# A trunk with a product-key expert layer: which gathered expert rows stand beside the choice of experts, and which engine takes them

## The reference, cut to what matters

```python
s = jnp.einsum('thpd,hpnd->thpn', q, sub_keys)
sv, si = lax.top_k(s, PEER_TOPK)
cand = (sv[:, :, 0, :, None] + sv[:, :, 1, None, :]).reshape(PEER_BLOCK, PEER_HEADS, PEER_TOPK * PEER_TOPK)
...
fs, fi = lax.top_k(cand, PEER_TOPK)
experts = jnp.take_along_axis(cidx, fi, axis=-1)
g = jax.nn.softmax(fs, axis=-1)
hid = jax.nn.gelu(jnp.einsum('td,thkd->thk', xb, u[experts]))
return jnp.einsum('thk,thkd->td', g * hid, v[experts])
```

## Time and profile before

| | us |
|---|---|
| median of three executions | 3921.12 |
| the profiled execution | 3898.55 |
| its span, first to last instruction | 3896.7 |
| VectorE busy | 2923.2 (75%) |
| TensorE busy | 2408.7 (62%) |
| GpSimd busy | 2397.6 (62%) |
| ScalarE busy | 531.2 (14%) |

### The profile page before, as it was taken

One profiled execution on the slowest core, in us unless ns is written; L12 is line 12 of the kernel. 1 busy time (PEld: TensorE's weight loads), 2 busy tenths in 40 slices (PEclk: granted clock), 3 DMA queues, 4 the chain that ended last, 5 costly groups with the idle time before them and its releaser, 6 DMA issues. The chain is left out here.

```text
span 3896.7 us, 29311 instructions
## 1 busy us (share of the span) xinstructions
PE 2408.7 (62%) x8928; PEld 1667.8 (43%) x8928; DVE 2923.2 (75%) x5647; ACT 531.2 (14%) x1237; POOL 2397.6 (62%) x2052
## 2 busy tenths in 40 slices
PE   8899527786798617767598717687788815600000
PEld 6676412464585313345486413355576513200000
DVE  2311786788877896778888797788777797798889
ACT  2310001122211101112110101122210101100000
POOL 0000377776675677766676577776566577777775
PEclk9989769997798859888698958998799968955555
DMA  4234699999899889999899989999799988999998
GB/s 176 96 107 140 213 324 361 369 392 348 294 408 409 339 316 347 368 384 392 325 389 409 352 321 347 361 390 391 291 365 409 370 323 308 355 350 367 368 387 339
DMA packets 359900, 1295.78 MB, mean 333 GB/s; under 512 B 40512, under 2 KB 40768, under 8 KB 359744
## 3 DMA queue, kind: packets, MB, share of 16 engines
q0 software_dynamic: 294912, 1073.87, 72.9%
q1 hardware_dynamic: 64256, 217.94, 14.8%
q10 hardware_dynamic: 576, 2.10, 0.1%
HBM read 1291.65 MB, written 2.10 MB: 332 GB/s over the span
## 5 line engine op out<-in xcount | busy, mean ns | idle before, releaser
L1057 POOL DMA_INDIRECT ring<-in_peer_u,eidx x1024 | 1222.6, 1194 | 960.1 <-DVE eidx L1181 475.1
L1057 POOL DMA_INDIRECT ring<-in_peer_v,eidx x1024 | 1174.8, 1147 | 516.8 <-issue 288.1
L1094 DVE CUSTOM_DVE_ANT_0 ring<-ring,hp 128x1024 f32<-128x1024 f32 x1024 | 1236.4, 1224 | 266.0 <-DMA ring<-in_peer_u,eidx 254.1
L1099 DVE SCALAR_TENSOR_TENSOR acc<-ring,wgt,acc 128x1024 f32<-128x1024 f32 x744 | 949.2, 1290 | 123.4 <-DMA ring<-in_peer_v,eidx 101.2
L519 PE MATMUL bank<-xt,panel 128*128 128x256 f32 x4096 | 952.8, 392 | 33.7 <-ACT raw L854 8.5
L519 PEld LDWEIGHTS bank<-xt,panel 128*128 128x128 f32 x4096 | 804.1, 198 | 164.0 <-issue 27.0
L752 PE MATMUL bank<-ring,dg 128*128 128x512 f32 x1120 | 549.6, 632 | 497.2 <-ACT dg L826 363.7
L752 PEld LDWEIGHTS bank<-ring,dg 128*128 128x128 f32 x1120 | 208.9, 198 | 825.4 <-issue 578.6
L594 PE MATMUL bank<-dg,ex 128*128 128x128 f32 x640 | 112.8, 349 | 149.2 <-DVE dg L1341 84.5
L594 PEld LDWEIGHTS bank<-dg,ex 128*128 128x128 f32 x640 | 105.4, 257 | 161.3 <-issue 145.7
L715 PE MATMUL bank<-yt,panel 128*128 128x256 f32 x768 | 173.6, 379 | 0.0
(11 more groups left out here) (164 smaller groups left out, 1884.0 us busy)
## 6 DMA issues: line engine op xcount, KB each, us to landing
panel<-in_panels SPq DMA_DIRECT2D x368, 512.0 KB
ring<-in_peer_u,eidx POOLq DMA_INDIRECT x1024
ring<-in_peer_v,eidx POOLq DMA_INDIRECT x1024
work<-in_rel_bias SPq DMA_DIRECT2D x16, 512.0 KB
gb<-in_ln_g SPq DMA_DIRECT2D x8, 512.0 KB
gb<-in_ln_b SPq DMA_DIRECT2D x8, 512.0 KB
panel<-in_keys SPq DMA_DIRECT2D x16, 256.0 KB
work<-in_x SPq DMA_DIRECT2D x4, 512.0 KB, 5.2
```

The lines of the kernel that those rows point to most:

```text
L1057: pool.indirect_dma_start(ring[:, n % RING, :], None, t_in["peer_u" if kind == "U" else "peer_v"], bass.IndirectOffsetOnAxis(ap=eidx[:, t, ...
L1094: v.tensor_tensor_reduce(row, row, hp[:, t, :], 1.0, 0.0, ALU.mult, ALU.add, hid[:, t, c:c + 1]).then_inc(used, 1)
L1099: stt(out=acc[:, t, :], in0=row, scalar=wgt[:, t, c:c + 1], in1=acc[:, t, :], op0=ALU.mult, op1=ALU.add).then_inc(used, 1)
```

## The change

Lanes 1 to 3 hold U rows of tile 0 of their own phase, 32 in each in phases 1 to 3, which VectorE dots with a copy of hp's tile 0 that ScalarE lays into PSUM (banks 4 and 5), and V rows of tile 1 of the phase before, which TensorE sums in banks 6 and 7. In phase 0 the lanes hold 40, 56 and 56 U rows, head by head and of both tiles; those of tile 0 use the PSUM copy. All other rows stand in the mixers, and what is left in the tail. The stream is written over phases: a V row may stand in the lanes after its own mixer. Sums are added once in a phase, for tile 1 alone, at the eighth row place of lane 3, followed by the layer norm of the phase before. Indices are kept for two phases. GELU and weights are made per head and tile.

```diff
+U_LANES = [(0, 40, 56, 56)] + [(0, 32, 32, 32)] * (PHASES - 1)
+V_LANES = [(0, 0, 0, 0), (0, 26, 26, 12)] + [(0, 40, 40, 16)] * (PHASES - 2)
+NORM_AT = 7
+def merged(a, b):
+    order = sorted([((2 * i + 1) * len(b), 0, i) for i in range(len(a))]
+                   + [((2 * i + 1) * len(a), 1, i) for i in range(len(b))])
+    return [(a, b)[j][i] for _, j, i in order]
...
+    rows, back = [], []
+    for p in range(PHASES):
+        n = sum(U_LANES[p])
+        if p:
+            u = of(p, "U", 0, range(HEADS)) + of(p, "U", 1, range(HEADS))
+        else:
+            u = [r for head in range(HEADS) for t in range(TILES) for r in of(p, "U", t, [head])]
+        lanes, u = u[:n], u[n:]
+        for it in range(1, LANES):
+            mine, lanes = lanes[:U_LANES[p][it]], lanes[U_LANES[p][it]:]
+            v, back = back[:V_LANES[p][it]], back[V_LANES[p][it]:]
+            beside = len(mine) // 2 if it == LANES - 1 and v else len(mine)
+            rows += merged(v, mine[:beside]) + mine[beside:]
+        v0, v1 = of(p, "V", 0, range(HEADS)), of(p, "V", 1, range(HEADS))
+        after = sum(V_LANES[p + 1]) if p + 1 < PHASES else 0
+        early = len(v1) - LAST // 2 - after if p + 1 < PHASES else 0
+        first = merged(v0[:len(v0) - LAST // 2], v1[:early])
+        rows += merged(first, u) + merged(v0[len(v0) - LAST // 2:], v1[early:early + LAST // 2])
+        back = v1[early + LAST // 2:]
+    rows += back
...
-LANE_ROWS = (0, 40, 64, 64)
-MIXER_ROWS = {"A": (16, 60), "B": (8, 32), "C": (12, 56), "G": (16, 64), "O": 16}
+LANE_ROWS = [[u + v for u, v in zip(U_LANES[s], V_LANES[s])] for s in range(PHASES)]
+MIXER_ROWS = [None, {"A": (12, 48), "B": (8, 28), "C": (8, 44), "G": (8, 60), "O": 16}] + [
+    {"A": (12, 52), "B": (8, 32), "C": (12, 48), "G": (12, 64), "O": 16}] * (PHASES - 2)
...
 def on_pe(n):
-    return kind == "V" and stage == "T" and (it > 1 or it == 0 and k % 2 == 1)
+    return kind == "V" and t == 1 and KEY_OF[n][1] == "T"
+def is_near(n):
+    return kind == "U" and t == 0 and KEY_OF[n][1] == "T"
...
+        hp_near = wide[2]
-        pa = bank[4:8]
+        pa = bank[6:8]
...
             def stage_a(s):
                 project_qk("A", s, 0)
                 project_qk("A", s, 1)
+                if s:
+                    pe.wait_ge(scores_read, s * LANES)
+                    pe.wait_ge(used, LAST_NEAR[s - 1] + 1)
+                if s > 1:
+                    pe.wait_ge(added, s - 1)
...
                 if s:
                     pe.wait_ge(tq_ev, s * 16)
-                    pe.wait_ge(added, 2 * s - 1)
                 turn(xn, bank[0:2], ready, x_turned, x_taken, s * 4)
                 pe.wait_ge(x_taken, s * 4 + 4)
-                if s:
-                    pe.wait_ge(scores_read, s * LANES)
...
                 take_turned(xt, bank[0:2], h_turned, h_taken, s * 4)
+                act.wait_ge(ln1_done, (s + 1) * TILES)
+                act.wait_ge(e_done["C"], (s + 1) * UNITS * 4)
+                copy(hp_near[:, :], hp[:, 0, :]).then_inc(hp_shown, 1)
                 queries(s, 0)
...
-                if kind == "U" and k == 0 and t == 0:
+                if kind == "U" and k == 0:
                     pool.wait_ge(peer_idx, s * LANES + head // 2 + 1)
...
-                        v.tensor_tensor_reduce(row, row, hp[:, t, :], 1.0, 0.0, ALU.mult, ALU.add, hid[:, t, c:c + 1]
+                        near = hp[:, t, :]
+                        if is_near(n):
+                            near = hp_near[:, :]
+                            if DVE_PLACE[n] == min(DVE_PLACE[m] for m in rows_of(key) if is_near(m)):
+                                dve.wait_ge(hp_shown, p + 1)
+                        v.tensor_tensor_reduce(row, row, near, 1.0, 0.0, ALU.mult, ALU.add, hid[:, t, c:c + 1]
...
                 def go():
-                    rows((s, "T", it, next(calls)))
+                    i = next(calls)
+                    rows((s, "T", it, i))
+                    if s and it == LANES - 1 and i == NORM_AT:
+                        add_sums(s)
+                        finish(s - 1)
...
                     choose(s, it)
-                    if it == 0 and s:
-                        add_sums(2 * s - 1)
-                        finish(s - 1)
                     gates(s, it)
-                add_sums(2 * s)
```

More of the change, by code:

```diff
@@ L84, with of @@
 CHOICES = 10
-def stream():
[L89 to L100, removed]
+U_LANES = [(0, 40, 56, 56)] + [(0, 32, 32, 32)] * (PHASES - 1)
[5 more added lines that the diff above has]
+    return [(a, b)[j][i] for _, j, i in order]
+def stream():
+    def of(p, kind, t, heads):
+        return [(p, kind, head, k, t) for head in heads for k in range(TOP)]
+    rows, back = [], []
[11 more added lines that the diff above has]
+            rows += merged(v, mine[:beside]) + mine[beside:]
+        assert not back
+        v0, v1 = of(p, "V", 0, range(HEADS)), of(p, "V", 1, range(HEADS))
[5 more added lines that the diff above has]
+    rows += back
+    assert len(rows) == PHASES * ROWS
     return rows
@@ L122, in row_plan @@
             for stage in "AC":
-                before, total = MIXER_ROWS[stage]
+                before, total = MIXER_ROWS[s][stage]
                 if stage == "C":
-                    early, later = MIXER_ROWS["B"]
+                    early, later = MIXER_ROWS[s]["B"]
                     for j, n in enumerate(spread(later, 2)):
@@ L137, in row_plan @@
         for it in range(1, LANES):
-            plan += [((s, "T", it, i), k) for i, k in enumerate(spread(LANE_ROWS[it], CHOICES))]
-    left = ROWS - sum(LANE_ROWS)
+            plan += [((s, "T", it, i), k) for i, k in enumerate(spread(LANE_ROWS[s][it], CHOICES))]
+    left = PHASES * ROWS - sum(k for _, k in plan)
     plan += [((PHASES, "Z", i, 0), k) for i, k in enumerate(spread(left, left // 8))]
@@ L154, in on_pe @@
 def on_pe(n):
-    kind, head, k, t = STREAM[n % ROWS]
-    s, stage, it, i = KEY_OF[n]
-    return kind == "V" and stage == "T" and (it > 1 or it == 0 and k % 2 == 1)
+    p, kind, head, k, t = STREAM[n]
+    return kind == "V" and t == 1 and KEY_OF[n][1] == "T"
+def is_near(n):
+    p, kind, head, k, t = STREAM[n]
+    return kind == "U" and t == 0 and KEY_OF[n][1] == "T"
 PE_SUMS = [n for n in range(PHASES * ROWS) if on_pe(n)]
@@ L163 @@
 DVE_PLACE = {n: i for i, n in enumerate(n for n in range(PHASES * ROWS) if n not in PE_PLACE)}
[L166 to L174, removed]
+SUM_ROWS = {s: [n for n in PE_SUMS if KEY_OF[n][0] == s] for s in range(1, PHASES)}
+LAST_NEAR = {s: max(DVE_PLACE[n] for n in DVE_PLACE if is_near(n) and KEY_OF[n][0] == s) for s in range(PHASES)}
+GELU_NO, WGT_NO = {}, {}
+for _p, _kind, _head, _k, _t in STREAM:
+    if _kind == "U" and _k == TOP - 1:
+        GELU_NO[(_p, _head, _t)] = len(GELU_NO)
+    if _kind == "V" and _k == 0:
+        WGT_NO[(_p, _head, _t)] = len(WGT_NO)
+for _s in range(1, PHASES):
+    assert SUM_ROWS[_s][-1] < RANGE[(_s, "T", LANES - 1, NORM_AT)][1]
 def rows_of(key):
@@ L817, in gelus @@
                 for n in rows_of(key):
-                    p, r = divmod(n, ROWS)
-                    kind, head, k, t = STREAM[r]
+                    p, kind, head, k, t = STREAM[n]
+                    cols = slice(head * TOP, (head + 1) * TOP)
                     if n in PE_PLACE:
@@ L1045, in _ @@
             for n in range(PHASES * ROWS):
[L1046 to L1048 removed]
+                s, kind, head, k, t = STREAM[n]
+                if kind == "U" and k == 0:
                     pool.wait_ge(peer_idx, s * LANES + head // 2 + 1)
```

66 lines of the change are left out of this document (29 added, 37 removed).

## The result

In the comparison that the prediction was made for, the changed kernel took 4068.06 us (median of four executions, 4064.2 to 4080.54) beside 3920.51 for the kernel before: a ratio of 1.0406, 95% interval 1.038 to 1.0433. Ratios with an interval are the record's; they can differ from the quotient of the two medians by up to 0.5% (the quotient is 1.0376 here). It is slower by 148 us where 50 were forecast, and 33 us above the range's upper end. The first windows by stage show where the time went. They run from the first row that VectorE takes to the last of lane 0, from there over lanes 1 to 3, and so on for phases 1, 2 and 3; the last is the tail. Columns as in the earlier trace rows.

The account below looks back on a forecast made before the run. VectorE was busy 75%, gathers set the pace in most mixer stages, VectorE in lane 1. Terms: +43 - 19 - 10 - 69 + 106 = +51, giving 3971 us on the median; range 3905 to 4035.

Parts of the forecast that it names:

- the lanes' term: Lanes 1 to 3, phases 2 and 3: 318 us a phase against 297, cost 43 for both.
- The third rival: Lanes: more V rows behind the queries, slot waits count in full; 62 us slower, 4033; chance 0.08.
- the queries' hold: Lanes: queries hold TensorE, so GpSimd waits for a slot; 4 us counted, up to 8.4 seen.
- the count of stops: GpSimd should wait for an index 13 times, twelve of them over 10 us, where before it was 4.
- the mixers' 69: Mixers with lane 0: rows that leave them give back 69 us in all, bounds 0 and 125.
- a stop: GpSimd waiting for a lane's index before new heads' U rows: 12.7 us each, nine more in phases 1 to 3.
- the 106: Tail: 416 rows instead of 344 take 582 us against 476, cost 106.
- the 1.33: Tail: the prediction is wrong if a row takes under 1.33 us.
- that rival: First rival, faster: VectorE, not DMA, sets the time nearly everywhere; nine stops cost 14 us; 3859; chance 0.11.
- The dot from PSUM does free GpSimd: Against the fourth rival: PSUM dots hold GpSimd as before, lanes 1 and 2 57 us slower, 4028; chance 0.05.
- The second: No change: rows stand fully in the mixers' chain, giving back 125 instead of 69; 3915; chance 0.16.
- The ceiling of 369 GB/s on reads: Fifth rival: long gathers in lanes 1 and 2 go at 369 GB/s, not 409; 57 us, 4028; chance 0.02.

Follow-up runs that it names:

- taking the queries' hold apart: Changed kernel with the five parts of the next lane's queries spread over row places 2 to 6 instead of all at place 3: 1.0057.
- the nine stops alone: Kernel before with only nine more GpSimd waits for a lane's index added, ahead of lanes, stage A and tail: 1.0229.
- more rows in lane 3: Changed kernel with V rows first and queries apart, plus four V rows each of lanes 1 and 2 moved to lane 3: 0.9948.

## Why the prediction was wrong

The changed kernel on all occasions on which it ran:

| occasion | kernel before, us | changed, us | ratio | VectorE's gaps at L1159 | lanes 1 to 3, phases 1, 2, 3 | tail |
|---|---|---|---|---|---|---|
| first | 3920.51 | 4068.06 | 1.0406 | 90.6 us | 315, 362, 359 | 593 |
| third, again | 3848.52 | 3904.17 | 1.0111 | none | 289, 322, 321 | 560 |
| fourth | 3860.91 | 3897.66 (one execution) | (1.0095) | none | 288, 324, 323 | 551 |
| fifth | 3854.67 | 3896.88 | 1.0093 | none | 287, 323, 322 | 551 |
| sixth | 3905.83 | 4060.8 | 1.0399 | 85.4 us | 312, 358, 359 | 596 |

Ratios are near 1.01 without gaps and 1.04 with them, and nothing between. The sum, step by step, in us of difference between profiled executions (first: 4069.1 against 3896.7; again: 3910.1 against 3870.7):

| step | predicted | first comparison | again, no late updates |
|---|---|---|---|
| phase 0 | -10 | -22 | -21 |
| mixers with lane 0 | -69 | -69 | -82 |
| lanes, phase 1 | -19 | +17 | -6 |
| lanes, phases 2 and 3 | +43 | +129 | +52 |
| tail | +106 | +117 | +96 |
| sum | +51 | +172 | +39 |

**The step that failed** is the lanes' term: "Lane 1 is 4.5 to the first landing, 71 x 1.28 = 91, panels ... and 4 for the queries". I took signals between engines as costing nothing when the DMA engines are full. In phase 3 of the first trace, lane 1 takes 127 us from first row to first row and lane 2 124, where the prediction has 113, and lane 3 with its boundary 97, where it has 85.5; without late updates the three are 111, 112 and 87. So the lane's own working holds in phase 3 (in phase 1 the lanes take 289 us without late updates, where it has 280). The surplus of the first comparison, 172 against 51, lies in the lanes: they are 122 us over their term, and the other steps cancel. Of the same kernel's lanes, 26, 40 and 38 us, 104 in all, come and go with the late updates between the first trace and the one "again". In lane 1 of phase 3, 11 of 16 us stand in the queries, from their first matmul to their last copy. That late updates make the whole of the 104 is inferred from such places, not shown by an experiment. The third rival had the right place, the queries' hold, and 62 us for it; it had the wrong mechanism for most of it, as the hold isn't longer because more rows stand behind it, but because TensorE's updates reach ScalarE late.

Why the kernel before pays less: its lanes are the same on both kinds of occasion. In them the gathers are slower beside dots from SBUF (1.99 us beside dots back to back, 1.20 in the mean of the lanes), it has fewer V rows behind TensorE, and GpSimd's next rows are there when an index is late. Which of these it is, if any, was not told apart. It too loses some 50 us in all, 3906 to 3921 against 3849 to 3861; its tail takes 476 and 482 us with late updates, 464 and 442 without.

**Right:** the count of stops (13 waits for an index), the gathers beside dots from PSUM at 0.94, the mixers' 69 within 13 us, the direction. **Off in size, and cancelling:** a stop costs 6 to 12 us, not 12.7, and taking the queries' hold apart gave 14 us back, all in phase 3, where six lanes at 4 us each were put down for it. Phase 0 gained 21, not 10: the dots from PSUM free GpSimd there too, which I had not put in; read from SBUF, they cost 11 of it. That the sum without late updates, 39, comes near the forecast's 51 is in part luck: all five steps are off by 9 to 13 us, and they cancel. The tail's surplus was 96 on one occasion, 109 on another (551 against 442) and 117 and 114 with late updates: the 106 was fair, but a row costs 1.28 to 1.43 us from execution to execution, not one price; on the fourth and fifth occasion the tail's 551 us are 1.32 a row, just under the 1.33 below which the prediction called itself wrong.

**The rivals.** VectorE doesn't set the time: the nine stops alone cost 53 us or more, where that rival has 14. The dot from PSUM does free GpSimd, by some 57 us. The second, that the mixers give everything back, fails on their 69 to 82 us. The ceiling of 369 GB/s on reads is not there: the tail held 388 GB/s over 560 us and the mixer with lane 0 of phase 2 387 over 558. The Trainium skill's figure of 358 GB/s ("DMA: Bandwidth & Descriptors", section "Bandwidth", under "Where 436 GB/s comes from") was passed on every occasion, with and without late updates. The same section gives it, a few lines above, as each core's share when both cores of a pair stream, and this kernel runs on one core.

**What stays open.** What makes updates late. They go with the occasion, never with the kernel alone: no execution of the changed kernel was between the two levels, and all kernels of one occasion showed them or none did. Whether it is the chip, what runs on its other cores or something else, no run here tells. The record numbers the chip 2 on the second, third and sixth occasion, and the sixth alone of these had them, so the number of the chip does not tell it. A rival that no run tests is the recording itself: the traces with late updates are the very ones that lack 24 to 36% of the semaphore updates, and no execution here was timed without its span and clock being recorded. The recording may have held the engines up, or one cause may have done both. That late updates need full DMA engines rests on the places where they stand (1.02 to 1.03 in the windows above), not on an experiment.

## What to carry to other kernels

Where one queue issues all transfers in order, the order counts more than the number: put work whose inputs are long there ahead of the first item that waits, and break up what holds the consumer of the queue; here this turned a loss of 1.1% into none, and into 1.0% faster than before with more rows in lane 3, the tail's dots from PSUM and half of its V rows of tile 1 on TensorE, on occasions without late updates. Idle time of the queue's engine is not the price: 206 us of it went, and the lanes gained 27. Time both kernels on more than one occasion before a few per cent are believed: the same pair gave 1.01 three times and 1.04 twice. In this case the schedule with many short hand-overs beside full DMA engines was hit harder than the one before. Look for waits with no releaser ("issue", "remote") before explaining a miss by the kernel, and for pages without times to landing, which show that records are missing; the trace that this prediction was made from had both.

## What the runs showed of the hardware

On two of six occasions semaphore updates and VectorE's own next instruction came late by 1 to 11 us while the DMA engines stood at a share of 1.02 to 1.03 and some 410 GB/s; on the other four they did not at the very same share. The traces with late updates also lack records, and the cause is open. A dot whose second input lies in PSUM costs VectorE the same (1218 against 1224 ns) and leaves GpSimd's gather at 0.94 us; from SBUF the mean gather in the lanes was 1.07 to 1.15. TensorE summed V rows that stand one behind another at 1.8 us a row in the tail (230.2 us busy for 128), slower than VectorE's 1.29; with every second row the gathers ran at 385 GB/s over the tail.
